# Out projections of four mixers, run by input chunk into eight open accumulators instead of by output chunk

## The chip, the core and the metric

The kernel is one program on one core of a Trainium2 chip. The metric is device time in microseconds (us) of the launch, lower is better. A core has TensorE (PE in the profile, with its weight loads as PEld), VectorE (DVE), ScalarE (ACT), GpSimd (POOL) and SyncE (SP), which here issues nearly all of the DMA transfers. Each engine works through its own instructions in the order in which they were written, and waits for others by semaphores only. So a wait holds back all that stands behind it on the same engine.

## The reference, cut to what matters

Ten blocks run one after the other on x, 256 tokens by 1024 channels in fp32: four mixers and six feed-forward blocks.

```python
# a mixer (first kind), residual included
h = rms_norm(x, gain)
proj = h @ w_in                       # queries, keys, values, gates of all heads
o_a = gqa_attention(...)              # six heads of 64
o_b = diff_attention(...)             # four heads of 96, then a norm per head
o_c = gated_linear_scan(...)          # four heads of 64, then a norm and a gate
mix = concat([o_a, o_b, o_c], -1)     # 1024 channels
x = x + mix @ w_out                   # the out projection, 1024 x 1024
# a feed-forward block
hf = rms_norm(x, gain) @ w_up
x = x + (act(gate(hf)) * val(hf)) @ w_down
```

The order of the blocks is mixer "mix1" (layer 0), feed-forward, "mix1" (layer 1), feed-forward, feed-forward, mixer "even" (a convolution branch with a layer norm, and eight attention heads), feed-forward, feed-forward, mixer "odd" (four pooling groups and eight attention heads), feed-forward.

## The kernel before, in words

x lies transposed in SBUF: eight chunks of 128 channels, each 128 partitions by 256 tokens. Every product is made exact enough for fp32 by splitting both sides in two: a value is its high part (`wh`, `hh`, `mh`) plus the rest (`wl`, `hl`, `ml`). ACT writes the high part, DVE the rest. Each 128x128 tile of weights is multiplied three times (L1130 to L1132: high by high, rest by high, high by rest).

Weights come in units. A unit of an out projection is 128 x 1024 values, so eight tiles and 24 matmuls. Units pass through a ring of four slots: SP loads `raw` (L351), ACT makes `wh` (L504), DVE makes `wl` (L744), and PE multiplies. `split_next(i + RING)` stands behind unit i in ACT's and DVE's order, and ACT waits there until PE has used unit i. So splits run four units ahead, into the next block too.

A mixer has 26, 14 or 16 units of input projection and then 8 of out projection. The table `W` gives the rest of a mixer's work: pairs of a piece and a number, each with the input unit after which it stands, and every engine writes its share of the pieces in that order. Pieces named in this document are `attn t` (on PE: turn the probabilities of head t-3, scores of head t, output of head t-4; on DVE: row maxima of head t, normalisation of head t-1, and for every second head the rest part `ml` of a finished chunk), `conv` (DVE taps of the convolution), `pool` (one matmul on PE, then `mh` on ACT, `ml` on DVE), `post` (in "mix1": norms of the B and C heads on DVE, ten transposes on PE, then `mh` and `ml` of chunks 3 to 7) and `ln` (in "even": layer norm of the convolution branch, then chunks 0 to 3). The pieces with the last number (26, 14 or 16) stand after all input units; nothing else is left for PE there.

Then comes the out projection. PE waits until all eight chunks of `ml` are there (`mix_lo` at `MIX_OUT`). It works by output: unit o takes all eight input chunks into bank `gb[o % 4]`. After each unit DVE adds the bank to x (L1038, semaphore `s_xo`), ACT forms `hh` of that chunk for the next block (`gain_hi`, L521) and DVE `hl` (`gain_lo`, L761), with the ring's split between. GpSimd, which waits for `s_xo` chunk by chunk, sums the squares of x for the next norm: a product and an addition for each chunk (L410 and L411, in `norm` of GpSimd), two instructions that follow each other by a wait.

The next block begins on PE with `first_unit`: its first unit, each of whose eight tiles waits for the `hl` of its chunk, and then a norm matmul (L1139) that waits for GpSimd's sum (`s_acc`). All later units stand behind that matmul on PE. `first_unit` itself starts when seven of the eight chunks of x are updated.

## Time and profile before

| what | value |
|---|---|
| device time, median of 3 runs | 1890.3 us (1887.63 to 1890.84) |
| span of the profiled execution | 1882.6 us (the profile lists no other time for it) |
| PE busy | 1712.7 us, 91% |
| DVE busy | 1230.0 us, 65% |
| ACT busy | 860.1 us, 46% |
| POOL busy | 495.1 us, 26% |
| mean DMA rate | 146 GB/s |

The span runs from the first to the last instruction. What lies around it is 7.7 us against the median. Busy shares are means over the whole program. A feed-forward block keeps PE busy nearly all the time, whereas each mixer has a stretch at its end, between the last input unit and the out projection, in which PE has little to do: 50 us in the first, from 151 us to 201 us. The row of the granted clock (PEclk) in 40 slices shows the same places as dips below 9.

### The profile page before, as it was taken

Reading aid. Unit: us, or ns where it says so; the run is one execution under the profiler, and the core shown is the slowest. Engines: PE = TensorE matmul, PEld = TensorE weight load, DVE = VectorE, ACT = ScalarE, POOL = GpSimd, SP = SyncE. Lnnn points to the kernel's source line nnn. Section 1 sums busy time; section 2 is a strip of 40 time slices with the busy share of each in tenths; the row PEclk is TensorE's granted clock in tenths of the full one; section 3 lists DMA queues with packets and bytes.
Section 4 is the critical chain, followed back from the end, with each engine's and each line's share of the span. In section 5 each row is a group of like instructions: output and inputs, shape, how many; then the busy total and the mean of one; then the engine's idle time right before and its main releaser. Section 6 shows DMA issues by size and latency. Waiting matters only on the chain. (4 is left out here: it accounts for less than half of the span.)

```text
span 1882.6 us, 35550 instructions
## 1 busy us (share of the span) xinstructions
PE 1712.7 (91%) x13260; PEld 1625.1 (86%) x13260; DVE 1230.0 (65%) x1750; ACT 860.1 (46%) x1250; POOL 495.1 (26%) x511
## 2 busy tenths in 40 slices
PE   5887799999977999999999456999999999789999
PEld 5775799998856999999999435999999998579999
DVE  7677666657786766655557986655555556865553
ACT  3445355533543555444444243544354434435442
POOL 3040333310211433223320002333123311343320
PEclk9987899999986999999999757999999999899999
DMA  6330256644320556656654301566455654235563
GB/s 223 101 112 23 90 170 178 222 161 135 102 67 23 159 179 194 198 164 179 196 200 135 101 1 56 177 182 215 164 168 180 212 179 145 67 101 179 179 214 99
DMA packets 70800, 274.25 MB, mean 146 GB/s; under 512 B 7872, under 2 KB 9024, under 8 KB 70592
## 3 DMA queue, kind: packets, MB, share of 16 engines
q1 hardware_dynamic: 70272, 271.04, 46.3%
q0 software_dynamic: 448, 2.13, 0.3%
q8 instruction: 52, 0.85, 0.2%
q14 instruction: 28, 0.23, 0.0%
HBM read 272.09 MB, written 1.05 MB: 145 GB/s over the span
## 5 line engine op out<-in xcount | busy, mean ns | idle before, releaser
L744 DVE TENSOR_TENSOR wl<-raw,wh 128x1024 fp32r<-128x1024 f32 (+1 forms) x474 | 632.5, 1335 | 299.5 <-ACT wh L504 298.7
L1130 PE MATMUL gb<-hh,wh 128*128 128x256 f32 x2768 | 802.4, 290 | 26.3 <-DVE wl L744 17.0
L1131 PE MATMUL gb<-hl,wh 128*128 128x256 f32 x2768 | 788.6, 285 | 0.0
L1132 PE MATMUL gb<-hh,wl 128*128 128x256 f32 x2768 | 787.9, 285 | 0.0
L504 ACT ACTIVATE wh<-raw 128x1024 fp32r<-128x1024 f32 (+1 forms) x474 | 528.5, 1118 | 343.7 <-PE gb L1132 339.6
L1130 PEld LDWEIGHTS gb<-hh,wh 128*128 128x128 f32 x2768 | 536.6, 194 | 41.6 <-DVE wl L744 17.0
L1131 PEld LDWEIGHTS gb<-hl,wh 128*128 128x128 f32 x2768 | 536.9, 194 | 3.2 <-issue 2.9
L1132 PEld LDWEIGHTS gb<-hh,wl 128*128 128x128 f32 x2768 | 536.6, 194 | 0.0
L1131 PE MATMUL gb<-gul,wh 128*128 128x256 f32 x1056 | 298.7, 283 | 0.0
L1132 PE MATMUL gb<-guh,wl 128*128 128x256 f32 x1056 | 298.3, 282 | 0.0
L1130 PE MATMUL gb<-guh,wh 128*128 128x256 f32 x1056 | 296.5, 281 | 1.8 <-POOL gul L493 1.7
L493 POOL TENSOR_TENSOR gul<-gu,guh 128x256 f32 x132 | 164.1, 1243 | 298.8 <-ACT guh L677 298.8
L1130 PEld LDWEIGHTS gb<-guh,wh 128*128 128x128 f32 x1056 | 200.7, 190 | 2.6 <-POOL gul L493 2.1
L1132 PEld LDWEIGHTS gb<-guh,wl 128*128 128x128 f32 x1056 | 198.2, 188 | 0.0
L1131 PEld LDWEIGHTS gb<-gul,wh 128*128 128x128 f32 x1056 | 197.6, 187 | 0.0
L490 POOL TENSOR_TENSOR tap<-tap,rstd 128x256 f32<-128x256 f32 x132 | 120.0, 909 | 200.3 <-ACT tap L674 109.9
L410 POOL TENSOR_TENSOR sq<-x 128x256 f32<-128x256 f32 x70 | 52.0, 742 | 254.4 <-DVE x L1091 229.2
L670 ACT ACTIVATE tap<-gs 128x256 f32<-128x256 f32 x88 | 36.8, 418 | 154.4 <-DVE gs L1058 154.3
L521 ACT ACTIVATE hh<-x,prm 128x256 fp32r<-128x256 f32 (+1 forms) x80 | 39.7, 504 | 129.5 <-DVE x L1091 129.3
L1130 PE MATMUL gb<-mh,wh 128*128 128x256 f32 x256 | 76.2, 298 | 12.7 <-DVE ml L887 9.1
L761 DVE SCALAR_TENSOR_TENSOR hl<-x,prm,hh 128x256 fp32r<-128x256 f32 (+1 forms) x80 | 59.9, 756 | 41.5 <-ACT hh L521 41.5
L1058 DVE TENSOR_TENSOR gs<-gb,rstd 128x256 f32<-128x256 f32 x132 | 55.8, 423 | 38.8 <-PE gb L1132 38.2
(190 smaller groups left out, 1666.5 us busy)
## 6 DMA issues: line engine op xcount, KB each, us to landing
raw<-in_wa SPq DMA_DIRECT2D x378, 512.0 KB, 3.6
raw<-in_wb SPq DMA_DIRECT2D x96, 704.0 KB, 4.1
x<-in_x SPq DMA_DIRECT2D x1, 1024.0 KB, 4.9
out_x<-x SPq DMA_DIRECT2D x8, 128.0 KB, 3.1
row<-in_row POOLq DMA_DIRECT2D x1, 836.0 KB, 10.6
tab<-in_bias SPq DMA_DIRECT2D x3, 256.0 KB, 4.4
con<-in_const POOLq DMA_DIRECT2D x1, 544.0 KB, 7.7
tab<-in_bias SPq DMA_DIRECT2D x1, 512.0 KB, 4.8
```

Source lines behind the costliest of these rows:

```text
L410: link(nc.gpsimd.tensor_tensor(sq[:, 0:SEQ], xc, xc, ALU.mult))
L490: nc.gpsimd.tensor_tensor(tap[:, j, :], tap[:, j, :], rstd[:, :], ALU.mult).then_inc(s_up, 1)
L493: nc.gpsimd.tensor_tensor(gul[:, part], gu[:, j, :], guh[:, part].bitcast(f32), ALU.subtract).then_inc(s_gul, 1)
L504: nc.scalar.activation(wh[:, slot, 0:nt * P], raw[:, slot, 0:nt * P], ACT.Copy).then_inc(s_hi, 1)
L521: nc.scalar.activation(hh[:, part], x[:, part], ACT.Copy, scale=prm[:, at0]).then_inc(s_hh, 1)
L670: nc.scalar.activation(tap[:, j, :], gate, ACT.Silu).then_inc(s_tap, 1)
L744: nc.vector.tensor_tensor(wl[:, slot, 0:nt * P], raw[:, slot, 0:nt * P], wh[:, slot, 0:nt * P].bitcast(f32), ALU.subtract).then_inc(s_lo, 1)
L761: nc.vector.scalar_tensor_tensor(out=hl[:, part], in0=x[:, part], scalar=prm[:, at0], in1=hh[:, part].bitcast(f32), op0=ALU.mult, op1=ALU. ...
L1058: nc.vector.tensor_tensor(gs[:, j, 1:SEQ + 1], gb[2 * j][:, 0:SEQ], rstd[:, :], ALU.mult).then_inc(s_gs, 1)
L1130: nc.tensor.matmul(bank, a, rhs_h(k), start=start and k == 0, stop=False)
L1131: nc.tensor.matmul(bank, a, rhs_l(k), start=False, stop=False)
L1132: last = nc.tensor.matmul(bank, b, rhs_h(k), start=False, stop=stop and k == nt - 1)
```

## The change

The out projection is turned round. A unit is now one input chunk: 128 rows of `w_out` with all 1024 output columns. It is multiplied into eight accumulators, one for each output chunk, that stay open over all eight units. Four PSUM banks hold two accumulators each (`sums_of`). A unit can run as soon as its own chunk of `mh` and `ml` is there. `OUT_CHUNKS` gives the order of the chunks, and new pieces `kout` (multiply a unit) and `ksplit` (the ring's split that belongs behind it) place units among the attention pieces: three of eight in "mix1", four in "even", seven in "odd". The other units follow at the end. No output is complete before the last unit. That unit signals after each output (`s_ko`), and the eight updates of x, with their `hl`, follow each other on DVE there. The transposes of `post` go to the `mb` banks, since `gb` holds the accumulators.

```diff
+        OUT_CHUNKS = {"mix1": [0, 1, 2, 3, 4, 5, 6, 7], "even": [4, 5, 6, 7, 0, 1, 2, 3], "odd": [0, 4, 1, 5, 6, 2, 7, 3]}
...
-                     [(26, "attn", t) for t in range(8, 14)] + [(26, "post", 0)],
+                     [(26, "attn", 8), (26, "kout", 0), (26, "attn", 9), (26, "ksplit", 0), (26, "kout", 1), (26, "attn", 10),
+                      (26, "ksplit", 1), (26, "kout", 2), (26, "attn", 11), (26, "ksplit", 2), (26, "attn", 12),
+                      (26, "attn", 13), (26, "post", 0)],
...
+        def sums_of(o):
+
+            return gb[o % 4][:, o // 4 * SEQ:(o // 4 + 1) * SEQ]
...
# ACT, mixer
+                for r in range(placed(kind, "ksplit"), DC - 2):
+                    split_next(U0[n] + nin + r + RING)
                 for o in range(DC):
-                    split_next(U0[n] + nin + o + RING)
                     gain_hi(n + 1, o)
+                    if o in (DC - 3, DC - 1):
+                        split_next(U0[n] + nin + DC - 2 + o // (DC - 1) + RING)
...
# DVE, mixer
-                for o in range(DC):
-                    u = nin + o
-                    dve.wait_ge(s_pe, U0[n] + u + 1)
-                    xc = x[:, o * SEQ:(o + 1) * SEQ]
-                    nc.vector.tensor_tensor(xc, gb[o % 4][:, 0:SEQ], xc, ALU.add).then_inc(s_xo, 1)
-                    split_next(U0[n] + u + RING)
-                    gain_lo(n + 1, o)
+                for r in range(placed(kind, "ksplit"), DC - 2):
+                    split_next(U0[n] + nin + r + RING)
+                for o in range(DC + 1):
+                    if o < DC:
+                        if o < DC - 1:
+                            dve.wait_ge(s_ko, K0[n] + o + 1)
+                        else:
+                            dve.wait_ge(s_pe, U0[n + 1])
+                        xc = x[:, o * SEQ:(o + 1) * SEQ]
+                        nc.vector.tensor_tensor(xc, sums_of(o), xc, ALU.add).then_inc(s_xo, 1)
+                    if o >= 1:
+                        gain_lo(n + 1, o - 1)
+                for r in (DC - 2, DC - 1):
+                    split_next(U0[n] + nin + r + RING)
...
# PE
+            def out_chunk(m, n, kind, r):
+
+                i, c = U0[n] + IN_UNITS[kind] + r, OUT_CHUNKS[kind][r]
+                slot = i % RING
+                pe.wait_ge(s_lo, i + 1)
+                pe.wait_ge(m["mix_lo"], 3 + (1, 1, 2, 2, 3)[r - 3] if kind == "mix1" and r >= 3 else r + 1)
...
+                for o in range(DC):
+                    if r == DC - 1 and o >= 4:
+                        pe.wait_ge(s_xo, DC * n + o - 3)
+                    a, b = wh[:, slot, o * P:(o + 1) * P], wl[:, slot, o * P:(o + 1) * P]
+                    bank = sums_of(o)
+                    nc.tensor.matmul(bank, a, mc(mh, c), start=r == 0 and o < 4, stop=False, skip_group_check=True)
+                    nc.tensor.matmul(bank, a, mc(ml, c), start=False, stop=False, skip_group_check=True)
+                    last = nc.tensor.matmul(bank, b, mc(mh, c), start=False, stop=r == DC - 1, skip_group_check=True)
+                    if o == DC - 1:
+                        last.then_inc(s_pe, 1)
+                    elif r == DC - 1:
+                        last.then_inc(s_ko, 1)
...
-                pe.wait_ge(m["mix_lo"], MIX_OUT[kind])
-                for o in range(DC):
-                    i = U0[n] + nin + o
-                    if o >= 4:
-                        pe.wait_ge(s_xo, DC * n + o - 3)
-                    tiles(i, i % RING, gb[o % 4][:, 0:SEQ], DC, lambda k: mc(mh, k), lambda k: mc(ml, k), True, True)
+                for r in range(placed(kind, "kout"), DC):
+                    out_chunk(m, n, kind, r)
```

DVE at the end of the first mixer, before the change. L999 is the last `ml`, L1038 the update of x, L744 a split, L761 an `hl`, L796 the reciprocal of the next norm. The three rows from L1038 to L761 stand there eight times.

```order
L999 TENSOR_TENSOR ml<-gb,mh 128x512 x2
L999 TENSOR_TENSOR ml<-gb,mh 128x256
L1038 TENSOR_TENSOR x<-gb,x 128x256
L744 TENSOR_TENSOR wl<-raw,wh 128x1024
L761 SCALAR_TENSOR_TENSOR hl<-x,prm,hh 128x256
...
L796 RECIPROCAL rstd<-rstd 128x256
```

DVE at the same place with the change; L1022, L1068, L767, L784 and L819 are the same five operations.

```order
L1022 TENSOR_TENSOR ml<-mb,mh 128x256
L767 TENSOR_TENSOR wl<-raw,wh 128x1024 x3
L1068 TENSOR_TENSOR x<-gb,x 128x256 x2
L784 SCALAR_TENSOR_TENSOR hl<-x,prm,hh 128x256
...
L1068 TENSOR_TENSOR x<-gb,x 128x256
L784 SCALAR_TENSOR_TENSOR hl<-x,prm,hh 128x256 x2
L767 TENSOR_TENSOR wl<-raw,wh 128x1024 x2
L819 RECIPROCAL rstd<-rstd 128x256
```

Splits no longer stand between the updates of x: three stand ahead of the first update and two behind the last `hl`.

DVE near the end of mixer "even", before the change: normalisation of a head (L934), the last taps of the convolution (L852, L856), two `ml` (L965), and the first addition of `ln` (L860).

```order
L934 TENSOR_SCALAR pr<-pr,small 128x256 [waits vector_step]
L934 TENSOR_SCALAR pr<-pr,small 128x256
L852 SCALAR_TENSOR_TENSOR y<-qq,prm,y 128x256
L852 SCALAR_TENSOR_TENSOR y<-qq,prm,y 128x256 [waits vector_step] x6
L856 TENSOR_TENSOR y<-y 128x256 [waits vector_step]
L965 TENSOR_TENSOR ml<-mb,mh 128x256 [waits even0_mix_hi,vector_step]
L965 TENSOR_TENSOR ml<-mb,mh 128x256 [waits even0_mix_hi]
L860 TENSOR_TENSOR acc<-y 128x256
```

The same place with the change (L957, L875, L879, L988, L883; L767 is a split):

```order
L957 TENSOR_SCALAR pr<-pr,small 128x256 [waits vector_step]
L957 TENSOR_SCALAR pr<-pr,small 128x256
L767 TENSOR_TENSOR wl<-raw,wh 128x1024 [waits w_hi_ready]
L875 SCALAR_TENSOR_TENSOR y<-qq,prm,y 128x256
L875 SCALAR_TENSOR_TENSOR y<-qq,prm,y 128x256 [waits vector_step] x6
L879 TENSOR_TENSOR y<-y 128x256 [waits vector_step]
L988 TENSOR_TENSOR ml<-mb,mh 128x256 [waits even0_mix_hi,vector_step]
L767 TENSOR_TENSOR wl<-raw,wh 128x1024 [waits w_hi_ready]
L988 TENSOR_TENSOR ml<-mb,mh 128x256 [waits even0_mix_hi]
L767 TENSOR_TENSOR wl<-raw,wh 128x1024 [waits w_hi_ready]
L883 TENSOR_TENSOR acc<-y 128x256
```

Three splits, each of which waits for its ACT half, now stand ahead of the layer norm, and one of them ahead of the last taps.

PE near the end of mixer "odd", before the change: pooling matmuls (L1309), turned probabilities (L1219), outputs of heads (L1243).

```order
L1309 MATMUL mb<-at,poolw 128x256 [waits odd0_probsT,odd0_pooled]
L1219 MATMUL mb<-con,pr 128x128 [waits odd0_mix_lo,odd0_probs]
...
L1243 MATMUL mb<-ptb,tv 64x256 [waits odd0_probsT,odd0_v_tokens]
...
L1309 MATMUL mb<-at,poolw 128x256 [waits odd0_probsT,odd0_pooled]
L1219 MATMUL mb<-con,pr 128x128 [waits odd0_mix_lo,odd0_probs]
...
L1130 MATMUL gb<-mh,wh 128x256 [waits w_lo_ready,odd0_mix_lo]
```

The same place with the change (L1343, L1251, L1275); each row L1361 is the first of the 24 matmuls of a unit.

```order
L1361 MATMUL gb<-mh,wh 128x256 [waits chunk_projected,odd0_mix_lo,w_lo_ready]
...
L1343 MATMUL mb<-at,poolw 128x256 [waits odd0_probsT,odd0_pooled]
L1251 MATMUL mb<-con,pr 128x128 [waits odd0_mix_lo,odd0_probs]
...
L1361 MATMUL gb<-mh,wh 128x256 [waits odd0_mix_lo,w_lo_ready]
...
L1361 MATMUL gb<-mh,wh 128x256 [waits odd0_mix_lo,w_lo_ready]
...
L1343 MATMUL mb<-at,poolw 128x256 [waits odd0_probsT,odd0_pooled]
```

Whole units of 24 matmuls now stand between the pooling and attention steps.

## Rows read from the trace of the kernel before

**Rows 1.** The page's costliest groups: busy us, mean ns of one, idle before.
```profile
L744 DVE TENSOR_TENSOR wl<-raw,wh 128x1024 fp32r<-128x1024 f32 (+1 forms) x474 | 632.5, 1335 | 299.5 <-ACT wh L504 298.7
...
L504 ACT ACTIVATE wh<-raw 128x1024 fp32r<-128x1024 f32 (+1 forms) x474 | 528.5, 1118 | 343.7 <-PE gb L1132 339.6
```

**Rows 2.** Timeline, PE, second mixer's out projection: start us, us, engine, line.
```profile
598.18 0.58 PE L1130 MATMUL gb<-mh,wh 128*128 128x256 f32 x1 [1.32 <-DVE ml L999]
...
602.97 0.28 PE L1130 MATMUL gb<-mh,wh 128*128 128x256 f32 x1
...
605.84 0.28 PE L1130 MATMUL gb<-mh,wh 128*128 128x256 f32 x1
```

**Rows 3.** Timeline, ends of the first and second mixer, DVE and PE.
```profile
188.99 1.49 DVE L972 TENSOR_TENSOR y<-y 128x1280 f32<-128x1280 f32 x1 [6.53 <-ACT y L577]
...
199.12 0.69 DVE L999 TENSOR_TENSOR ml<-gb,mh 128x512 fp32r<-128x512 f32 x1 [1.84 <-ACT mh L620]
...
201.05 0.58 PE L1130 MATMUL gb<-mh,wh 128*128 128x256 f32 x1 [1.32 <-DVE ml L999]
...
586.12 1.49 DVE L972 TENSOR_TENSOR y<-y 128x1280 f32<-128x1280 f32 x1 [6.02 <-ACT y L577]
```

**Rows 4.** Timeline, first mixer's last chunk and the next block's first unit.
```profile
226.53 0.28 PE L1130 MATMUL gb<-hh,wh 128*128 128x256 f32 x1
...
229.66 0.79 POOL L411 TENSOR_TENSOR acc<-acc,sq 128x256 f32<-128x256 f32 x1
```

**Rows 5.** Norm matmuls behind the mixers: ns min/median/max, first and last start us.
```profile
L1139 PE MATMUL mb<-acc,con x2: 379/431/483, 230.5 to 230.8; 128*128 128x256 f32 x2
...
L1139 PE MATMUL mb<-acc,con x2: 378/378/379, 627.3 to 627.5; 128*128 128x256 f32 x2
...
L1139 PE MATMUL mb<-acc,con x2: 379/431/483, 1182.6 to 1182.9; 128*128 128x256 f32 x2
...
L1139 PE MATMUL mb<-acc,con x2: 379/431/483, 1691.9 to 1692.2; 128*128 128x256 f32 x2
```

**Rows 6.** Timeline, start of the program: DVE and GpSimd on eight ready chunks.
```profile
8.73 6.53 DVE L761 SCALAR_TENSOR_TENSOR hl<-x,prm,hh 128x256 fp32r<-128x256 f32 x8 [8.73 <-ACT hh L521]
...
7.15 0.72 POOL L411 TENSOR_TENSOR acc<-acc,sq 128x256 f32<-128x256 f32 x1
...
11.06 0.68 POOL L410 TENSOR_TENSOR sq<-x 128x256 f32<-128x256 f32 x1
...
12.68 0.68 POOL L410 TENSOR_TENSOR sq<-x 128x256 f32<-128x256 f32 x1
...
17.47 1.59 POOL L411 TENSOR_TENSOR acc<-acc,sq 128x256 f32<-128x256 f32 x1
```

**Rows 7.** DVE's instructions on x: ns min/median/max, first and last start us.
```profile
L761 DVE SCALAR_TENSOR_TENSOR hl<-x,prm,hh x80: 476/834/965, 8.7 to 1690.4; 128x256 fp32r<-128x256 f32 x60, - x20
...
L1038 DVE TENSOR_TENSOR x<-gb,x x32: 410/411/426, 206.6 to 1688.9; 128x256 f32<-128x256 f32 x32
```

**Rows 8.** Stretches: us, busy (x) of PE, PEld, DVE, ACT, POOL, PEclk, DMA, GB/s.
```profile
32.00:36.00 4.00, 4.00 (x20) 3.76 (x20) 3.14 (x2) 0.69 (x1) 0.00 (x0) 0.57 0.73 242
...
570.00:575.00 5.00, 5.00 (x13) 2.83 (x14) 4.75 (x13) 3.86 (x12) 0.00 (x0) 0.50 0.01 2
```

**Rows 9.** Timeline, mixer "even", DVE and PE ahead of the out projection.
```profile
1130.44 2.85 DVE L852 SCALAR_TENSOR_TENSOR y<-qq,prm,y 128x256 f32<-128x256 f32 x7
...
1136.39 0.41 DVE L860 TENSOR_TENSOR acc<-y 128x256 f32<-128x256 f32 x1
...
1151.50 1.43 DVE L887 TENSOR_TENSOR ml<-y,mh 128x256 fp32r<-128x256 f32 x4
...
1152.98 0.58 PE L1130 MATMUL gb<-mh,wh 128*128 128x256 f32 x1 [9.13 <-DVE ml L887]
```

**Rows 10.** Timeline, mixer "odd", PE ahead of the out projection.
```profile
1655.57 1.22 PE L1309 MATMUL mb<-at,poolw 128*128 128x256 f32 x2
...
1664.80 0.39 PE L1130 MATMUL gb<-mh,wh 128*128 128x256 f32 x1 [0.93 <-DVE ml L965]
```

More of the change, by code:

```diff
@@ L333, in group_of, with placed @@
             return max(g for g, (c0, _, _) in enumerate(qk_groups(kind, l)) if c0 <= c)
+        def placed(kind, what):
+            return sum(w == what for _, w, _ in W[kind])
+        K0 = [(DC - 1) * sum(is_mix[:n]) for n in range(NPH)]
         T0 = [16 * sum(is_mix[:n + 1]) for n in range(NPH)]
@@ L619, in do @@
                         act.wait_ge(m["mix_psum"], k + 2)
-                        nc.scalar.activation(mc(mh, c, w), gb[(0, 1, 3)[k]][:, 0:w * SEQ], ACT.Copy).then_inc(m["mix_hi"], 1)
+                        nc.scalar.activation(mc(mh, c, w), mb[(0, 1, 3)[k]][:, 0:w * SEQ], ACT.Copy).then_inc(m["mix_hi"], 1)
                 elif what == "sig":
@@ L631, in do @@
                         nc.scalar.activation(mc(mh, c), yc(2 * c), ACT.Copy).then_inc(m["mix_hi"], 1)
+                elif what == "ksplit":
+                    split_next(U0[n] + IN_UNITS[kind] + g + RING)
                 elif what == "pool":
@@ L1018, in do @@
                     layer_norm(m)
+                elif what == "ksplit":
+                    split_next(U0[n] + IN_UNITS[kind] + g + RING)
                 elif what == "pool":
@@ L1296, in do @@
                                 at0 = (c - 3 + cc) * P
[L1297 removed]
+                                last = nc.tensor.transpose(mb[(0, 1, 3)[k]][:, cc * SEQ + tile * P:cc * SEQ + (tile + 1) * P],
                                                            tmo[:, tile, at0:at0 + P], ident)
@@ L1305, in do @@
                     nc.tensor.matmul(MISC[:, 0:SEQ], ones, acc[:, :], start=True, stop=True).then_inc(m["ln_sum"], 1)
+                elif what == "kout":
+                    out_chunk(m, n, kind, g)
                 elif what == "pool":
```

24 lines of the change are left out of this document (17 added, 7 removed).

## The prediction, made before the changed kernel had been run

> **What bounds the kernel now.** I read the page's busy shares first: PE at 91% of the span is the bound of the program, and no other engine is near it. So the change can only give back what PE loses at the ends of the four mixers. Then I read, for each mixer, the timeline from the last input unit to the first unit of the next block, one engine at a time. The reader is to see four things there.
>
> First, the pace. At full clock a unit of 24 matmuls takes 605.84 - 602.97 = 2.87 us; the first unit of the same out projection took 602.97 - 598.18 = 4.79 us, since PE had been nearly idle and ran at half clock [rows 2]. In the first mixer the eight units took 226.53 - 201.05 = 25.48 us, so its first unit took 25.48 - 7 x 2.88 = 5.3 us [rows 3, 4].
>
> Second, what ends the wait ahead of the out projection. In "mix1" it is DVE: the work of `post` begins on it at 188.99, the first `ml` ends at 199.12 + 0.69 = 199.81, and PE starts at 201.05 after the last one [rows 3]. In "even" it is DVE's layer norm, begun at 1136.39, which ends in the four `ml` from 1151.50 on [rows 9]. In "odd" PE waits in short pieces only.
>
> Third, the end of the out projection. Updates of x come one per unit there, so GpSimd's sum of squares keeps step, and after the last update only one pair is left: its last addition ends at 229.66 + 0.79 = 230.45 and the norm matmul starts at 230.5 [rows 4, 5]. I call T the start of the last unit. Before, T = 226.53 - 2.88 = 223.65, and the norm matmul comes at T + 6.9, which is the time of the last unit and of the next block's first. PE loses 1 us at most.
>
> Fourth, the one place where this kernel works on eight ready chunks at once, the start of the program. It shows what the closing will be like. DVE's eight `hl` took 6.53 us, 0.82 each, and GpSimd's pairs (a product, an addition) came 12.68 - 11.06 = 1.62 us apart [rows 6].
>
> **The closing, the same in all four mixers.** After the change no output is complete before the last unit. Its first output can be read 3 matmuls of 0.12 us and the 0.28 us of a matmul's own time after its start, at T + 0.6. The update takes 0.41 us [rows 7]; with the semaphore GpSimd starts at T + 1.1. It needs one product of 0.6 us and seven pairs. DVE needs per chunk about 0.36 for the update and 0.82 for `hl`, 1.18 us, less than GpSimd's 1.62, so GpSimd sets the end. DVE's last `hl` ends at about T + 10.3, and then come two splits of weights [rows 1]. While DVE runs a split, an instruction of GpSimd takes twice as long (1.59 against 0.72 us), and `hl` costs it some 10% [rows 6]. So: T + 1.1 + 0.7 + 7 x 1.62 = T + 13.1 without the splits; at T + 10.3 there are 2.8 us left, the two splits, 1.7 us each when contended, cover 3.4 us in which GpSimd does 1.7 us of work, and 1.1 us remain: T + 14.8. The norm matmul starts at T + 14.9. It was T + 6.9. All later units stand behind it on PE, so each closing costs 8.0 us. Nothing hides it: PE has the last unit and one more, 5.8 us of work, in these 14.9 us.
>
> The bounds of this step: GpSimd uncontended (0.61 + 0.72 + two gaps of 0.08 = 1.49 us a pair) gives T + 12.3, a cost of 5.4; every pair contended by a split's factor at some point of it (2.2 us) gives T + 17.3, a cost of 10.4. I take 8.0, since the start of the program is nearest.
>
> The next block's first unit is no term of its own. It waits for seven updates, at about T + 7.3, and for the last `hl` at T + 10.3, so it ends at T + 10.7, still ahead of the norm matmul.
>
> The Trainium skill states in "SBUF — State Buffer", section "Who interferes with whom", that a DVE instruction with two inputs in SBUF and a GpSimd instruction that reads SBUF take turns, the second one fully blocked until the first ends. The splits in this trace agree (1.59 against 0.72 us), the `hl` beside GpSimd do not: pairs at 1.62 us leave no room for two `hl` of 0.48 us each. What it would give if it held for `hl` too is the second rival below.
>
> **The clock.** Between T + 10.7 and T + 14.9 PE does nothing, and before that it works in bits. In the trace PE stood still for about 2.7 us at 28.5 to 31.3, and the stretch after it shows a granted clock of 0.57, where half is 0.5: about 3.5 us at half speed, in which 0.093 us a matmul are lost [rows 8]. A whole unit at half clock costs 5.3 - 2.9 = 2.4 us [rows 2 to 4]. So each closing costs 0 to 2.4 us more, and I take 1.9. PE has three more units behind the norm matmul whose weights are ready or become so, before as after, so it is PE that is late, and the cost shows in full.
>
> **The gains, mixer by mixer, as a new T.**
>
> *First mixer.* Three units leave the end. They run among the attention pieces, where PE's work is on the way to DVE's: unit 0 stands ahead of the scores of the last head. It takes about 3.5 us and DVE needed those scores almost at once. DVE's own splits, 1.2 to 1.3 us each, and ACT's, 1.1 us, stand in that chain too [rows 1]. Followed step by step through the three engines, the last head's output and with it `post` come 1.6 us later than 188.99. Between zero (all hidden) and 3 x 2.87 + 3 x 1.3 = 12.5 us (nothing hidden) I take 1.6, because DVE has 6.5 us of idle time ahead of `post` [rows 3]. Unit 3 then needs only the first `ml`, 1.2 us earlier than before. T = 199.85 + 1.6 + 5.3 + 3 x 2.88 = 215.4 against 223.65, and the norm matmul at 230.3 against 230.5: -0.2 us.
>
> *Second mixer.* The same, but PE is at half clock in the whole stretch around unit 0 [rows 8], so the unit takes up to 5 us there and DVE waits 3 us more: 4.6 us for 1.6. T = 598.18 - 1.2 + 4.6 + 4.8 + 3 x 2.88 = 615.0, norm matmul at 629.9 against 627.3: +2.6 us.
>
> *Mixer "even".* Four units leave the end, but three splits enter DVE's chain ahead of the layer norm. The first waits for its ACT half, which stands behind the probabilities turned on PE, behind unit 0: it ends at about 1133.6, where the taps began at 1130.44, 3.2 us. The second adds its length and the wait for a head's output behind unit 1, 2.6 us together, and the third 1.9 us. The layer norm starts at 1136.4 + 7.7 = 1144.1 [rows 9]. Ends: 0, and 3 x (1.3 + 1.1) + 4 x 2.87 = 18.7 us with nothing overlapped. Unit 4 starts after the first of four `ml`: 1151.9 + 7.7 = 1159.6. T = 1159.6 + 5.5 + 2 x 2.88 = 1170.9 against 1152.98 + 5.5 + 6 x 2.88 = 1175.8, and the norm matmul at 1185.8 against 1182.6: +3.2 us.
>
> *Mixer "odd".* Seven units leave the end, but PE had only about 4.5 us of idle time between 1655.57 and 1664.80 [rows 10]. Unit 0 starts after the attention step that ends at 1655.6, half of it at half clock, and ends at 1659.3; with the two pooling rounds, which now wait behind whole units, and 7 units, PE reaches the last one at 1655.6 + 3.7 + 6 x 2.88 + 5.1 (attention and pooling matmuls) + 2.7 (waits for `ml` and `mh` of the pooling) = 1684.4. Before it was 1664.80 + 7 x 2.88 = 1684.96. The norm matmul comes at 1699.3 against 1691.9: +7.4 us.
>
> **Terms of no cost.** Matmuls: 24 a unit as before. The DMA of a unit is 512 KB as before, and slots fall free earlier. ACT's splits and `hh` fit beside DVE's work in the closing (1.06 and 0.5 us against 1.18 a chunk). The other banks for `post` move nothing.
>
> **The sum.** -0.2 + 2.6 + 3.2 + 7.4 = 13.0 us, and four times 1.9 for the clock, 7.6 us: 20.6 us. Against the profiled span of 1882.6 that is 1903.2, and with the 7.7 us that lie around it before (median 1890.3) it is 1911 us.
>
> **Rivals.**
>
> *The gain wins, faster than before.* The mechanism is PE's idle time in the attention tails: it takes the moved units whole, DVE's chain isn't touched, and the closing runs at GpSimd's own pace without loss of clock. Then the norm matmuls come at 213.8 + 12.3, 610.4 + 12.3, 1163.2 + 12.3 and 1680 + 12.3, which is -4.4, -4.6, -7.1 and +0.4: 1890.3 - 15.7 = 1875 us. For it: PE's idle time ahead of the out projections is real. Against it: DVE had no gap when unit 0 would run. It decides where the closing costs less than the units taken out, that is under 8.6 us in "mix1". In "odd" no closing is cheap enough.
>
> *The lock.* If every `hl` held GpSimd up for its own 0.48 us [rows 7], a pair would take 1.97 us and the two splits their 1.23 us each: T + 1.8 + 7 x 1.97 + 2.5 = T + 18.1, 3.2 us more in each closing, 1911 + 13 = 1924 us. For it: GpSimd's doubled instructions beside splits. Against it: the program's start.
>
> *The units don't run early.* If the waits at the units' heads (`mix_lo`, all input chunks read, weights split) came late, T stayed where it was and only the closings were left: 4 x (8.0 + 1.9) = 40, 1930 us. Against it: chunks 0 and 1 are finished well ahead of their units.
>
> **How the numbers follow.** The forecast has 70 of 100, the gain 8, the lock 10, late units 4, and 8 lie between the gain and the forecast, where the clock holds or the tails hide more. The forecast's own range is 1899 to 1924: without the clock's loss 1903, with both bounds partly met the rest. With the others I give 1895 to 1928. Within 0.2% (3.8 us), about what a measurement of this kernel can tell from no change, lies little: 0.05. Faster 0.09, slower 0.86.
>
> **What would show it.** In the profile after, GpSimd's seven pairs behind each mixer follow each other without gaps at 1.6 to 2.2 us, and PE's norm matmul starts behind GpSimd's last addition, 14 to 16 us after the last unit began, with a gap ahead of it of over 3 us. PEclk falls behind it. The group of matmuls on `mh` waits less for DVE in sum. DVE's layer norm in "even" starts 6 to 9 us later than before, counted from the last input unit. In "odd" the out projection's last unit begins within 2 us of before. The prediction is wrong if the norm matmul comes within 10 us of T, or if the wait ahead of it falls on another engine, or if `post` is delayed by more than 6 us.

## The result and the profile after

| | kernel before | changed kernel |
|---|---|---|
| median, us (lowest to highest, runs) | 1888.97 (1884.68 to 1890.84, 4) | 1898.07 (1897.32 to 1900.05, 4) |
| ratio to before, 95% interval | 1 | 1.0048 [1.0036, 1.0061] |
| profiled execution: span, us | 1882.6 | 1896.9 |

The change makes the kernel 9.1 us slower. The forecast had 1911 us, a loss of 20.6 us: the sign is right, the size more than double. The measured 1898.07 us lies 1 us below the forecast's own range (1899 to 1924) and inside the wider one (1895 to 1928).

The busy times and the granted clock come first, from the page of the changed kernel:

```profile
span 1896.9 us, 35564 instructions
...
PE 1716.3 (90%) x13260; PEld 1629.6 (86%) x13260; DVE 1220.9 (64%) x1750; ACT 858.3 (45%) x1250; POOL 478.1 (25%) x511
...
PEclk9988799999978899999999668999999999789999
...
L767 DVE TENSOR_TENSOR wl<-raw,wh 128x1024 fp32r<-128x1024 f32 (+1 forms) x474 | 629.6, 1330 | 320.9 <-ACT wh L522 320.5
```

No engine does other work than before (the splits answer to [rows 1]: 629.6 against 632.5 us). What changed is when things happen, so the closing of a mixer is what to read. The norm matmuls, which answer to [rows 5]:

```profile
L1171 PE MATMUL mb<-acc,con x2: 635/716/796, 229.8 to 230.4; 128*128 128x256 f32 x2
...
L1171 PE MATMUL mb<-acc,con x2: 635/714/793, 625.7 to 626.3; 128*128 128x256 f32 x2
...
L1171 PE MATMUL mb<-acc,con x2: 635/716/796, 1183.9 to 1184.5; 128*128 128x256 f32 x2
...
L1171 PE MATMUL mb<-acc,con x2: 634/714/793, 1703.4 to 1704.0; 128*128 128x256 f32 x2
```

Each takes 0.64 to 0.80 us where it took 0.38 to 0.48, so PE is at half clock in all four; the granted clock over the 2 us behind each is 0.50. The timeline of the first one says why (start, us, engine, line; in brackets the idle time and what ended it):

```profile
215.19 0.28 PE L1363 MATMUL gb<-mh,wl 128*128 128x256 f32 x1
...
229.83 1.22 PE L1171 MATMUL mb<-acc,con 128*128 128x256 f32 x2 [4.21 <-POOL acc L429]
```

```profile
216.37 0.61 POOL L426 TENSOR_TENSOR acc<-x 128x256 f32<-128x256 f32 x1 [55.46 <-DVE x L1068]
217.06 0.76 POOL L428 TENSOR_TENSOR sq<-x 128x256 f32<-128x256 f32 x1
217.90 0.80 POOL L429 TENSOR_TENSOR acc<-acc,sq 128x256 f32<-128x256 f32 x1
218.78 0.67 POOL L428 TENSOR_TENSOR sq<-x 128x256 f32<-128x256 f32 x1
...
224.34 1.59 POOL L429 TENSOR_TENSOR acc<-acc,sq 128x256 f32<-128x256 f32 x1
226.01 1.47 POOL L428 TENSOR_TENSOR sq<-x 128x256 f32<-128x256 f32 x1
...
229.06 0.72 POOL L429 TENSOR_TENSOR acc<-acc,sq 128x256 f32<-128x256 f32 x1
```

GpSimd runs its fifteen instructions one behind the other, 0.1 us apart at most, from 216.37 to 229.78, and PE waits 4.21 us for the last. The two that take 1.59 and 1.47 us run beside DVE's two splits (223.72, 3.30 us). The last unit began at T = 215.3, so the norm matmul comes at T + 14.5 (before: T + 6.9).

To see where the 14.3 us between the two spans lie, I cut each trace at its norm matmuls. A piece runs from the norm matmul of one block to that of the next, the last one to the end of the span; all in us. Two pieces between blocks of feed-forward alone are 190.5 in every trace but for 0.1 us and are left out.

| trace | mix1 | block behind | mix1, second | behind | even | behind | odd | behind |
|---|---|---|---|---|---|---|---|---|
| before | 208.3 | 192.9 | 203.9 | 192.9 | 171.9 | 190.6 | 128.2 | 190.7 |
| before, run again | 208.4 | 192.8 | 203.4 | 192.8 | 172.8 | 190.5 | 131.7 | 190.8 |
| changed | 207.2 | 193.4 | 202.5 | 193.5 | 174.2 | 192.2 | 136.8 | 193.5 |
| changed, run again | 211.4 | 193.4 | 203.2 | 193.5 | 175.3 | 193.1 | 135.7 | 193.0 |
| all units late | 213.4 | 193.3 | 210.0 | 193.4 | 169.2 | 192.0 | 138.4 | 193.2 |
| squares on ACT | 201.8 | 192.7 | 197.2 | 193.7 | 170.9 | 190.5 | 131.3 | 190.6 |
| PE kept busy | 208.1 | 193.2 | 202.7 | 193.5 | 175.3 | 192.2 | 137.1 | 190.7 |
| kept busy longer | 209.2 | 192.8 | 205.0 | 193.0 | 175.7 | 190.6 | 135.6 | 190.7 |
| units ahead of post | 205.6 | 193.3 | 200.3 | 193.5 | 171.0 | 192.8 | 137.7 | 193.5 |
| fastest kernel | 192.0 | 194.5 | 193.6 | 194.7 | 160.9 | 191.4 | 131.5 | 190.6 |

So by the two first traces the change costs 2.3 us in "even" and 8.6 in "odd", gives 1.1 and 1.4 in the two "mix1", and costs 0.5, 0.6, 1.6 and 2.8 in the blocks behind. The start moves by 0.4. How firm is this? Both traces of the changed kernel against both of the kernel before give +4.0 to +8.6 in "odd", +1.4 to +3.4 in "even", -1.4 to -0.2 in the second "mix1", -1.2 to +3.1 in the first, and 5.5 to 6.1 in the four blocks behind. "Odd", "even" and the blocks behind the mixers carry the loss; for the first mixer the sign isn't shown.

### The profile page after: what moved, and what is told of

Read it like the earlier page. It is cut to its first block and busy times, and to the rows that moved or that the text cites. A ratio compares the mean times of both kernels' runs of the same rounds, so it can differ in the third digit from the quotient of the medians.

```text
span 1896.9 us, 35564 instructions
## 1 busy us (share of the span) xinstructions
PE 1716.3 (90%) x13260; PEld 1629.6 (86%) x13260; DVE 1220.9 (64%) x1750; ACT 858.3 (45%) x1250; POOL 478.1 (25%) x511
## 5 line engine op out<-in xcount | busy, mean ns | idle before, releaser
L767 DVE TENSOR_TENSOR wl<-raw,wh 128x1024 fp32r<-128x1024 f32 (+1 forms) x474 | 629.6, 1330 | 320.9 <-ACT wh L522 320.5
L1162 PEld LDWEIGHTS gb<-hh,wh 128*128 128x128 f32 x2768 | 544.2, 197 | 46.1 <-DVE wl L767 17.3
L1163 PEld LDWEIGHTS gb<-hl,wh 128*128 128x128 f32 x2768 | 544.1, 197 | 3.5 <-issue 2.9
L1164 PEld LDWEIGHTS gb<-hh,wl 128*128 128x128 f32 x2768 | 543.6, 196 | 0.0
L508 POOL TENSOR_TENSOR tap<-tap,rstd 128x256 f32<-128x256 f32 x132 | 119.7, 907 | 203.2 <-ACT tap L697 110.3
L1361 PE MATMUL gb<-mh,wh 128*128 128x256 f32 x256 | 78.2, 305 | 10.7 <-DVE ml L910 8.2
L784 DVE SCALAR_TENSOR_TENSOR hl<-x,prm,hh 128x256 fp32r<-128x256 f32 (+1 forms) x80 | 52.1, 662 | 44.0 <-ACT hh L539 44.0
## 6 DMA issues: line engine op xcount, KB each, us to landing
row<-in_row POOLq DMA_DIRECT2D x1, 836.0 KB, 10.3
```

What stands on the lines that cost most here:

```text
L508: nc.gpsimd.tensor_tensor(tap[:, j, :], tap[:, j, :], rstd[:, :], ALU.mult).then_inc(s_up, 1)
L767: nc.vector.tensor_tensor(wl[:, slot, 0:nt * P], raw[:, slot, 0:nt * P], wh[:, slot, 0:nt * P].bitcast(f32), ALU.subtract).then_inc(s_lo, 1)
L784: nc.vector.scalar_tensor_tensor(out=hl[:, part], in0=x[:, part], scalar=prm[:, at0], in1=hh[:, part].bitcast(f32), op0=ALU.mult, op1=ALU. ...
L1162: nc.tensor.matmul(bank, a, rhs_h(k), start=start and k == 0, stop=False)
L1163: nc.tensor.matmul(bank, a, rhs_l(k), start=False, stop=False)
L1164: last = nc.tensor.matmul(bank, b, rhs_h(k), start=False, stop=stop and k == nt - 1)
```

## The experiments

The theory: what is given up is the closing (GpSimd's sums start late and end late, and PE's clock falls), and what is gained is the placement of units in the attention tails. The rivals: that the placement gains nothing or costs, and that the clock alone is the loss.

**The kernel before, unchanged.** No edit; it gives the scatter of the pieces.

> The kernel before once more, unchanged, as a measure of what its own runs scatter by. Its four runs so far lie between 1884.7 and 1890.8 us and its profiled span of 1882.6 us belongs to one of them. Both theories: ratio 1.000 with an interval that holds 1, and the interval between its norm matmuls (the ten PE matmuls of the sums of squares) equal within 0.5 us to those of the first trace. If the scatter sits in one block, the trace shows which.

Measured: 1890.02 us (11 runs), ratio 1.0003 [0.9994, 1.0012]; profiled span 1886.2. All pieces but one agree within 0.9 us. "Odd" takes 131.7 us against 128.2, and the granted clock differs there: 1.6 of the 3.5 us are there by 1640, behind a stretch (1630 to 1635) with 1.00 in the first trace and 0.75 in this one, and the rest comes in the ten us below, where the first trace has the higher clock again. The stretches of the first trace, then of this one (us, busy of PE, PEld, DVE, ACT, POOL, then PEclk):

```profile
1655.00:1660.00 5.00, 3.82 (x14) 1.68 (x12) 0.62 (x2) 1.43 (x3) 0.00 (x0) 0.79 0.01 3
1660.00:1665.00 5.00, 2.89 (x15) 1.55 (x14) 1.33 (x3) 1.49 (x4) 0.00 (x0) 1.00 0.00 0
```

```profile
1655.00:1660.00 5.00, 3.86 (x10) 1.66 (x8) 2.12 (x6) 1.07 (x2) 0.00 (x0) 0.50 0.00 0
1660.00:1665.00 5.00, 3.79 (x11) 1.97 (x12) 0.91 (x2) 1.45 (x3) 0.00 (x0) 0.68 0.00 0
```

The execution from which I had read every term was thus a short one: its span was 1882.6, when executions of the kernel before have a median time of 1889 us, a span of about 1887.

**All units at the end.** The changed kernel with every early out-projection unit and split taken out of the table. The accumulators and the closing stay.

```
-  [(26, "attn", 8), (26, "kout", 0), (26, "attn", 9), (26, "ksplit", 0), (26, "kout", 1), ...
+  [(26, "attn", 8), (26, "attn", 9), (26, "attn", 10), (26, "attn", 11), (26, "attn", 12), ...
```

> The change without its early units: all eight units of each out projection follow at the end, by input chunk, into the eight accumulators. Theory SUM (the closing costs: GpSimd's sum of squares starts with the last unit and the norm matmul waits for it, 14.4 us after that unit began against 6.9 before; the early units give time back): the last unit starts where it did in the kernel before, so 4 x 7.5 us and the half clock behind it, 5.5 us in sum: 35 us slower than before, about 1924 us, and so 26 us slower than the changed kernel. Rival TAIL (the early units and their splits make the attention stretches longer and that is the loss, the closing is cheap): no slower than the changed kernel, 1889 to 1898 us.

Measured: 1907.98 us, ratio 1.0102 [1.0086, 1.0117]. The early placement is worth about 10 us, and the turn without any early unit costs 19 us, not the 35 of the expectation or the 40 of my rival. The pieces show the parts: against the second run of before, the two "mix1" lose 5.0 and 6.6, "odd" 6.7, and "even" gains 3.6. In "mix1" unit 0 needs only its own chunk and starts 10.4 us behind the start of `post` (199.19, 188.80) where the whole out projection started 12.1 us behind it [rows 3]. That takes 1.7 us off each closing's 7.6. The gain in "even" I had overlooked. There the first units need only the attention's heads. These units stand ready behind PE's last layer-norm matmul and run while DVE still works on the layer norm:

```profile
1155.03 1.22 PE L1337 MATMUL mb<-acc,con 128*128 128x256 f32 x2 [4.02 <-DVE acc L894]
1155.69 0.78 PE L1361 MATMUL gb<-mh,wh 128*128 128x256 f32 x1
```

```profile
1156.79 1.75 DVE L896 RECIPROCAL rstd<-rstd 128x256 f32<-128x256 f32 x1 [1.82 <-ACT rstd L644]
...
1163.90 1.43 DVE L910 TENSOR_TENSOR ml<-y,mh 128x256 fp32r<-128x256 f32 x4
```

The changed kernel has spent these four units earlier, with three splits in DVE's chain, and PE then waits 8.21 us for the layer norm. Its table is 5.0 us worse in "even" (174.2 against 169.2) than no early unit there at all.

**Squares on ACT.** The changed kernel; behind a mixer ACT squares each chunk as it comes, and GpSimd only adds: seven instructions for fifteen.

```
+  def square_chunk(n, c):           # ACT, behind each hh
+      dst = acc[:, :] if c == 0 else sq[:, (c % 2) * SEQ:(c % 2 + 1) * SEQ]
+      nc.scalar.activation(dst, x[:, c * SEQ:(c + 1) * SEQ], ACT.Square).then_inc(s_sqa, 1)
...
+  ins = nc.gpsimd.tensor_tensor(acc[:, :], acc[:, :], sq[:, (c % 2) * SEQ:(c % 2 + 1) * SEQ], ALU.add)
```

> The changed kernel, with the eight squares of the sum behind each mixer made by ScalarE (0.5 us each, beside its 0.5 us hh), so that GpSimd only adds (0.8 us a chunk). Nothing is left out. Theory SUM: GpSimd ends with the last hl, the norm matmul comes about 10 us after the last unit began instead of 14.4: 4 x 4.4 = 18 us less than the changed kernel and some 3 us less of half clock, 1877 to 1882 us. Rival TAIL: within 2 us of the changed kernel, 1898. Rival HL (DVE's hl would end the closing anyway): the gap ahead of the norm matmul closes but the first unit's wait for hl takes its place, at most 2 us a mixer, 1890.

Measured: 1873.81 us, ratio 0.9924 [0.9911, 0.9938]. In the ratios that is 23 us less than the changed kernel. GpSimd's whole closing in this trace:

```profile
216.19 4.25 POOL L426 TENSOR_TENSOR acc<-acc,sq 128x256 f32<-128x256 f32 x5 [56.87 <-ACT sq L556]
221.01 1.62 POOL L426 TENSOR_TENSOR acc<-acc,sq 128x256 f32<-128x256 f32 x2 [0.57 <-ACT sq L556]
```

```profile
L1189 PE MATMUL mb<-acc,con x2: 379/380/380, 223.8 to 224.0; 128*128 128x256 f32 x2
```

GpSimd ends at 222.63 and the norm matmul comes at 223.8, 10.2 us behind the start of the last unit at 213.6, at full clock (0.38 us). GpSimd no longer sets this end. PE's next first unit does: it starts with the seventh update of x and fills the time up to the norm matmul, 4.5 us, since its first half runs at half clock (0.42 us a matmul).

```profile
219.36 0.40 PE L1180 MATMUL gb<-hh,wh 128*128 128x256 f32 x1 [2.01 <-DVE x L1086]
```

In the second mixer, at full clock, the norm matmul comes 9.1 us behind the last unit (604.58, 613.70). The four closings are 4.3 to 5.4 us shorter, 18 us in all. Three of the four blocks behind are back at 192.7, 190.5 and 190.6; the second stayed at 193.7 with a granted clock of 1.00 throughout, which I did not follow. With the control below this shows that GpSimd's sums set the end of each closing in the changed kernel.

**The same on the kernel before.** A control for the last one: are the squares on ACT a gain by themselves?

> The kernel before, its out projection by output, with the same eight squares behind each mixer on ScalarE as in the run that made them so for the change. Theory SUM: updates come one per 2.9 us here, so the sum was never late; the norm matmul moves by less than 1 us in each mixer, 1886 to 1889 us. Rival: squares on ScalarE are a gain of their own, in any kernel; then 15 us faster than before, as the changed kernel with them.

Measured: 1885.94 us, ratio 0.9989 [0.9976, 1.0001]. In the kernel before GpSimd keeps step with the units [rows 4], and unloading it gives about 2 us, which the interval does not tell from nothing. Nearly all of the 23 us of the run above belong to the closing that the change made.

**PE kept busy in the closing.** The changed kernel with 16 matmuls that nobody reads ahead of the next block's first unit, and 28 behind it.

```
+  for _ in range(28):
+      nc.tensor.matmul(mb[0][:, 0:SEQ], mh[:, 0:P], ml[:, 0:SEQ], start=True, stop=True)
   norm(n)
```

> The changed kernel with 16 matmuls that nobody reads ahead of the first unit behind each mixer and 28 ahead of its norm matmul, so that PE isn't idle in the closing. They should end before the sum of squares does. Theory CLOCK (PE's clock falls in the closing and the blocks behind start at half clock, 0.5 + 0.6 + 1.6 + 2.8 = 5.5 us by the two traces): the granted clock stays at 1.0 behind the norm matmul, 4 to 6 us faster than the changed kernel, 1893 us. Rival: the blocks behind were late for another reason (splits that come late), then the clock stays up and the time doesn't change; 1898 us.

Measured: 1897.67 us, ratio 1.0044 [1.0030, 1.0058]: nothing. The 28 ended too early, and the clock fell all the same behind three of the four mixers:

```profile
626.14 1.22 PE L1171 MATMUL mb<-acc,con 128*128 128x256 f32 x2 [2.59 <-POOL acc L429]
```

```profile
624.00:626.00 2.00, 0.00 (x0) 0.00 (x0) 0.00 (x0) 0.00 (x0) 1.84 (x3) 0.93 0.79 229
626.00:628.00 2.00, 1.86 (x6) 1.68 (x7) 0.10 (x1) 0.47 (x1) 0.08 (x1) 0.50 0.15 61
```

Behind the fourth it held, and that block took 190.7 us instead of 193.5. The run was a miss as a test, since it did not hold what it was to hold, so the next one did it again with 46.

> The changed kernel with 16 and 46 instead of 16 and 28 matmuls that nobody reads in each closing. With 28 PE still stood for 2.6 us ahead of the norm matmul and the clock fell in three of four places; where it didn't, the block behind took 190.7 us and not 193.5. Theory CLOCK: with 46 the clock stays at 1.0 everywhere, the blocks behind take 192.8, 192.8, 190.5 and 190.6 us instead of 193.4, 193.5, 192.2 and 193.5, and unless the norm matmul now waits for PE (up to 0.5 us each) that is 4 to 6 us less than the changed kernel, 1893. Rival: the blocks stay as long, 1898.

Measured: 1897.10 us, ratio 1.0040 [1.0025, 1.0054]. Now PE waits 0.47 us, and the clock stays:

```profile
628.83 0.70 PE L1171 MATMUL mb<-acc,con 128*128 128x256 f32 x2 [0.47 <-POOL acc L429]
```

```profile
628.00:630.00 2.00, 1.53 (x12) 1.27 (x11) 0.00 (x0) 0.43 (x1) 0.73 (x1) 1.00 0.33 135
630.00:632.00 2.00, 2.00 (x20) 2.00 (x19) 1.89 (x2) 0.04 (x1) 0.00 (x0) 1.00 0.00 0
```

The four blocks behind take 192.8, 193.0, 190.6 and 190.7 us, together 5.5 less than in the changed kernel and the same as before. So the lost clock costs 5.5 us in the blocks behind, and the loss in the mixers stays without it. Yet the median gained only 1 us against the first measurement of the changed kernel (1.0048), and 3 us against the one made beside this run (1.0056, below), where 5 were expected; the intervals overlap. The mixers of this trace are 2.0, 2.5 and 1.5 us longer, and 1.2 shorter. In the second one the clock was lower already ahead of the early unit (0.50 from 560 to 570; the changed kernel's trace has 0.77 and 0.54). Whether the added matmuls caused that I did not test.

**Units directly ahead of `post`.** In "mix1" units 0 to 2 stand behind the last attention matmuls and ahead of `post`, their splits after it; "even" has no early unit; "odd" stays as changed.

```
-  [(26, "attn", 8), (26, "kout", 0), (26, "attn", 9), (26, "ksplit", 0), (26, "kout", 1), ...
+  [(26, "attn", 8), ... (26, "attn", 13), (26, "kout", 0), (26, "kout", 1), (26, "kout", 2), (26, "post", 0)],
```

> The changed kernel with its early units in other places: in mix1 the three units stand directly ahead of post's transposes on PE (where PE waits 8.8 us for DVE's norms) and their splits behind post; in even no unit and no split stands ahead of the layer norm, so the first four follow PE's part of it, while DVE still works on it. The odd mixer is as in the change. Theory PLACE (units and splits inside the attention chain delay what follows, 2.0 us and 2.4 us in the two mix1, 5.0 us in even by the difference between early and late units there): 9 us faster than the changed kernel, 1889 us, the intervals between norm matmuls 205, 200 and 169. Rival: the early units raise PE's clock in the attention stretch and that pays for their delay; then no gain in mix1 and only even's 5 us, 1893.

Measured: 1891.43 us (12 runs), ratio 1.0018 [1.0006, 1.0030]: 6 us less than the changed kernel, at the same closing, where 9 were expected. The pieces give 1.6, 2.2 and 3.2 us of it to the two "mix1" and to "even"; single pieces scatter by as much, so the sum is what is measured. The mechanism shows in the first mixer. First the changed kernel:

```profile
190.68 1.10 PE L1268 MATMUL mb<-tv,ptb 128*128 128x96 f32 x8 [0.55 <-ACT y L595]
200.60 2.40 PE L1329 MATMUL mb<-con,y 128*128 128x128 f32 x10 [8.81 <-DVE y L1018]
203.22 0.55 PE L1361 MATMUL gb<-mh,wh 128*128 128x256 f32 x1 [0.23 <-DVE ml L1022]
```

then this one:

```profile
188.60 1.10 PE L1265 MATMUL mb<-tv,ptb 128*128 128x96 f32 x8 [0.51 <-ACT y L592]
...
198.52 1.31 PE L1326 MATMUL mb<-con,y 128*128 128x128 f32 x10 [0.17 <-DVE y L1015]
200.69 0.36 PE L1358 MATMUL gb<-mh,wh 128*128 128x256 f32 x1 [0.85 <-DVE ml L1019]
```

The units fill the 8.81 us in which PE stood still while DVE worked on `post`. PE waits 0.17 us behind them, so they delay nobody by much, and PE comes to the matmuls of `post` at full clock: 1.31 us against 2.40 for the same ten.

**Both together, and one step on.** First the two last edits in one kernel; then in addition the last three units of each mixer output by output again (for each output the three chunks), so that x comes in pieces of 9 matmuls and no longer all at once; then "odd" out as in the kernel before.

```
+  for o in range(DC):
+      for r in range(DC - LAST, DC):      # LAST = 3
+          slot, c = (i0 + r) % RING, OUT_CHUNKS[kind][r]
+          ... three matmuls on bank o ...
```

> The changed kernel with both: squares on ScalarE and the early units ahead of post and behind the layer norm. If the two effects are apart (one is in the closing, one ahead of the last units), they add: 1873.8 - 9 = 1865 us. If the attention stretch was hidden behind something else, 1870 or more.

Measured: 1864.73 us, ratio 0.9870 [0.9852, 0.9887], where 1865 was expected if the two effects add.

> As the one with squares on ScalarE and the early units moved, and the last three units of each mixer run output by output (nine matmuls, 1.08 us, for each output) once all chunks are there; their ring slots are split again after the last output. Theory: outputs come at the pace of DVE's two instructions a chunk, so the closing takes 11 us from the start of the last three units, 5.4 us from the start of the last one, instead of 10.2: 4 x 4.8 = 19 us less than the kernel without it, less 1 to 2 us a mixer for weights that now come late, 1850 us. Rival RING: the next block's units 1 to 3 are split too late and PE waits for them, then half of it is lost, 1857.

Measured: 1858.94 us, ratio 0.9843 [0.9824, 0.9862]. It gives 5 us in the ratios where 15 were expected. Part of the miss is in the closings. Counted from the transposes of `post` to the norm matmul they are 4.3 and 4.4 us shorter in the two "mix1" (19.5 for 23.8 us in the first), and 5.3 in "even", counted from the second unit. (The whole piece of the first mixer is 8.9 us shorter, but 4.6 of these lie ahead of `post` or at the start, where the edit changed nothing.) In "odd" the closing is only 0.3 us shorter, for the last three units need the splits of all three at once, and PE waits for the last of them and then runs at half clock:

```profile
1651.06 0.58 PE L1397 MATMUL gb<-mh,wh 128*128 128x256 f32 x1 [2.68 <-DVE wl L783]
```

The blocks behind are longer by 1.9, 1.9, 1.0 and 1.4 us. The time is near that of the rival in the expectation (three slots of weights come free at once at the end, so their transfers and splits start late), but its wait shows only once behind the first mixer, and small:

```profile
215.97 0.39 PE L1178 MATMUL gb<-hh,wh 128*128 128x256 f32 x1 [0.27 <-DVE wl L783]
```

Counted in matmuls since the norm matmul, PE is 10 behind the kernel without this edit (1.2 us) after 15 us of that block and 18 behind after 75 us. So the lengthening is measured and placed, and its cause stays open.

> The fastest kernel so far (squares on ScalarE, units moved, the last three by output) with the odd mixer's out projection as before the change, by output at the end. Theory ODD (that mixer had no idle time of PE to give, so its turn can only cost): the interval over it 128 to 131.5 instead of 132.9 and the block behind it 190.6 instead of 192.0: 3 to 6 us less, 1853 to 1856. Rival: with the cheap closing its early units pay, and it gets slower, 1861.

Measured: 1856.20 us, ratio 0.9835 [0.9816, 0.9853], as expected; it is the fastest kernel here, 31 us ahead of before. The two intervals overlap, so the step from 0.9843 to 0.9835 is not told from none; in the traces "odd" and the block behind it take 2.8 us less (131.5 and 190.6 against 132.9 and 192.0).

**The changed kernel again.**

> The changed kernel once more, unchanged. The first trace of the kernel before had 128.2 us from the norm matmul ahead of the odd mixer to the one behind it, the repeated one 131.7. Theory BASE (the first trace of before caught a short execution of that mixer, and the changed kernel's are steady): 1.0045 to 1.0055 of before, and the interval over the odd mixer 136.8 within 0.7 us, over mix1 207.2 and 202.5, over even 174.2 within 0.5 us. Rival: the changed kernel scatters there as well, by 2 us or more.

Measured: 1900.07 us, ratio 1.0056 [1.0038, 1.0074]. The first mixer takes 211.4 us against 207.2, the others agree within 1.1. Again the clock differs ahead of the early units, first trace and then this one:

```profile
160.00:170.00 10.00, 6.92 (x44) 5.59 (x45) 7.39 (x14) 6.67 (x14) 0.91 (x1) 0.84 0.01 2
```

```profile
160.00:170.00 10.00, 9.04 (x36) 7.49 (x37) 5.61 (x14) 6.19 (x13) 1.04 (x1) 0.50 0.00 0
```

So a single mixer's piece is good to 4 us, and a block's to 1 us (193.1 against 192.2 behind "even"). The terms below are taken from the two first traces and hold no better than that; the four closings, at T + 14.5 each, and the blocks behind are steadier.

## Why the prediction was right in its sign and wrong in its size

**The closing: right.** "T + 14.8. The norm matmul starts at T + 14.9." It came at T + 14.5 in the first mixer, in "even" (1169.4, 1183.9) and in "odd" (1688.9, 1703.4). GpSimd sets the end, and the two splits double its instructions. My pair of 1.62 us is what it took (218.78 to 220.40). The lock is refuted as I had priced it: beside DVE's first six `hl`, which took 0.48 to 0.62 us, GpSimd took 0.67 to 0.80 us an instruction, and the end came at T + 14.5 and not T + 18.1. Only the last two `hl`, which follow each other, took 0.93 and 0.95 us, and there it is DVE that loses (GpSimd 0.61 and 0.79). My 0.82 us for every `hl` was too much. DVE's last one ended at T + 8.5 for my T + 10.3, which moved the two splits and hardly the end.

The Trainium skill states in "SBUF — State Buffer", section "Who interferes with whom", that a DVE instruction with two SBUF inputs and a GpSimd instruction that reads SBUF contend for a shared port pair, and that this is an exclusive lock. The trace agrees for the splits (1.59 and 1.47 against 0.72 and 0.61 us) and not for the first six `hl`, beside which GpSimd gave up 0.1 us.

**The gain in the second mixer: the step of the mechanism that failed most.** "PE is at half clock in the whole stretch around unit 0, so the unit takes up to 5 us there and DVE waits 3 us more: 4.6 us for 1.6." I took the stretch's clock [rows 8] as given. With the early unit in it the clock rose:

```profile
568.30 0.58 PE L1361 MATMUL gb<-mh,wh 128*128 128x256 f32 x1
...
571.83 0.60 PE L1251 MATMUL mb<-con,pr 128*128 128x128 f32 x4
572.36 1.14 PE L1240 MATMUL mb<-y 48*128 48x256 f32 x8
```

```profile
570.00:575.00 5.00, 5.00 (x37) 3.93 (x36) 3.76 (x11) 3.05 (x10) 0.00 (x0) 1.00 0.01 2
```

The unit took 3.5 us (568.30 to 571.83), and the eight score matmuls behind it 1.14 us; before, such a group took 2.09:

```profile
564.78 2.09 PE L1208 MATMUL mb<-y 48*128 48x256 f32 x8
```

This is no accident of one execution. In five traces with the early unit (two of the changed kernel, squares on ACT, PE kept busy, and busy longer) the group behind unit 0 takes 1.14 us in both "mix1", whatever the clock ahead of the unit, and the granted clock is 1.00 from there to the end of the attention. In the three traces of the by-output kernel the second mixer's stretch from 565 to 575 had 0.50 to 0.74.

The work of `post` began at 588.09 instead of 586.12 [rows 3], 2.0 us later and not 4.6. Counted from the group of matmuls two ahead of the unit (563.37 against 563.77) the unit's own delay is 2.4 us, and 2.3 between the two second traces. Then the first unit behind `post` took 3.5 us (599.06 to 602.55) where I had 4.8 [rows 2], since PE had not been idle for as long. Of the forecast +2.6 us, -1.4 was measured: 4.0 us of the error (2.8 by the two second traces, which have -0.2).

In the first mixer T came at 215.3 for my 215.4, but by two errors that cancel. The first unit behind `post` took 3.4 us (203.22 to 206.66) for my 5.3, and `post` began 3.3 us later for my 1.6. That its piece came out at -1.1 for -0.2 is the closing, 0.4 us shorter than forecast, and the start. Of the 3.3 us (192.25 against 188.99) 1.5 were there before unit 0 ran (the group of matmuls two ahead of it on `con` and `pr` begins at 167.58 against 166.12). The unit's own delay is then 1.8 us for my 1.6.

**"Even": right in size, wrong in what I compared.** +2.3 for +3.2. The three splits stand in DVE's chain where I had them (1130.53, 1135.83, 1142.18), and the layer norm began at 1143.33 for my 1144.1. Counted from the head's normalisation ahead of them (1126.57 against 1127.62) they delay it by 2.3, 3.9 and 1.8 us for my 3.2, 2.6 and 1.9, so part of the match is luck. What I missed is that no early unit at all would have been 5 us better.

**"Odd": right, within its scatter.** +8.6 for +7.4 against the trace that I had read; against the second trace of before it is +5.1. PE waits for the pooling's `ml` behind whole units, as I had it, 2.4 us in two waits for my 2.7:

```profile
1663.58 0.59 PE L1343 MATMUL mb<-at,poolw 128*128 128x256 f32 x2
1665.35 0.63 PE L1251 MATMUL mb<-con,pr 128*128 128x128 f32 x4 [1.18 <-DVE ml L1046]
...
1674.54 0.63 PE L1251 MATMUL mb<-con,pr 128*128 128x128 f32 x4 [1.18 <-DVE ml L1046]
```

**The clock: right in mechanism, too dear.** "Each closing costs 0 to 2.4 us more, and I take 1.9." Measured: 0.5, 0.6, 1.6 and 2.8, 5.5 in sum for my 7.6. "The cost shows in full" was wrong behind the two "mix1". The loss of clock is there (0.75 granted in the 8 us from 231 and from 627, against 0.85 from 1185), but only 0.5 and 0.6 us of it are left at the next norm matmul. The rest is made good later in the block, where the kernel before has waits of its own. Counted in matmuls since the norm matmul, the changed kernel is 21 behind (2.5 us at 0.12) from 10 to 75 us of the first block. From 75 to 130 us it does 44 in 5 us and the kernel before mostly 43; then the kernel before waits for GpSimd's `gul` and the changed one, being late, does not. At 140 us it is 4 behind, 0.5 us.

```profile
364.63 0.39 PE L1130 MATMUL gb<-guh,wh 128*128 128x256 f32 x1 [0.84 <-POOL gul L493]
```

```profile
364.40 0.39 PE L1162 MATMUL gb<-guh,wh 128*128 128x256 f32 x1
```

What holds the kernel before at 43 no wait in the profile names, and I did not count the other blocks.

**The base: a mistake of its own.** "Against the profiled span of 1882.6 that is 1903.2, and with the 7.7 us that lie around it before (median 1890.3) it is 1911 us." Nothing of that kind lies around a span. In every profiled execution time less span is 1.8 us (1898.68 and 1896.9; 1887.94 and 1886.2). The 7.7 us were 1.8 and the distance between a short execution, 1884.4 us by the same 1.8, and the median. With 1.8 in its place the same sum gives 1905.0 us, 16.0 above the kernel before and still too much.

**The account.** The span was forecast at 1903.2 and came at 1896.9. The terms give -0.9 ("mix1"), -4.0 (second), -0.9 ("even"), +1.2 ("odd"), -2.1 (clock), together -6.7, and +0.4 from the start: -6.3. The rest of the way from 20.6 to 9.1 us, 5.2 us, is the base, the largest single part: before's profiled execution was 4.6 us under its median (1884.4 and 1888.97), the changed kernel's 0.6 over it. The re-run of before has its "odd" 3.5 us longer.

**The rivals.** The closing decides the sign, as the gain's rival itself said ("under 8.6 us in mix1"): at 7.6 us the two "mix1" come out ahead by 1.1 and 1.4 in the first traces, while in the second traces the first is 3.0 behind and the second 0.2 ahead. With the closing cut by ACT the whole kernel is faster than before. The units did run early, so the last rival is out; its 40 us for four bare closings measured 19, since late units in "even" gain, unit 0 in "mix1" starts earlier, and the clock costs less. The signs that I had named came true: GpSimd's sums without gaps, the norm matmul 14 to 16 us behind T with a gap of over 3 us ahead of it, a falling clock, and a layer norm in "even" 7 to 8 us later.

## What to carry to other kernels

Running an accumulation by input instead of by output moves all outputs to its end. Before doing it, count what consumes the outputs one by one (here fifteen GpSimd instructions in a row) and cut that first: the same placement lost 9 us with the squares on GpSimd and gained 15 us with them on ACT. Fill the place where the engine waits longest and nobody waits for it (ahead of `post`), not the places between steps of a chain. Before adding a forecast shift to a median, run the unchanged kernel's profile a second time, or take time less span from one execution: this mistake was worth 5.2 us here, more than the error of any single term.

## What the runs showed of the hardware

- A stretch in which PE was 100% busy by the profile, with small matmuls (48 rows among them), had a granted clock of 0.50 [rows 8], and 0.66 in the same 5 us of the second trace. One unit of 24 dense matmuls in its place took 3.5 us and left it at 1.00, up to 590 at least.
- An idle time of PE of 4.2 to 5.4 us ahead of the norm matmul brought the granted clock to 0.50 each time, one of 2.6 us in three of four closings, and one of 0.5 us in none of four. The profile gives the clock, not the reason why the fourth held.
- The clock in a broken-up attention stretch differs between executions of one kernel (0.84 and 0.50 over the same 10 us), and that is worth 2.8 us at `post` (195.08 against 192.25 where it starts) and so 2.8 of the 4.2 us between those two first mixers.
- DVE's `hl` (two SBUF inputs, 256 wide) alternating with updates of x cost GpSimd 0.1 us an instruction; two `hl` in a row took 0.94 us each for 0.48 and left GpSimd at 0.61 and 0.79 us (closing of the first mixer).
